# Hybrid decoder trunk on one core: gates and branch projections with tokens as rows of the product, merged rows transposed on TensorE

## The chip, the cores and the metric

One core of a Trainium2 chip runs the whole kernel. The metric is device time in microseconds (us) from launch to end. The kernel before takes 838.35 us (median of 3 runs, 837.55 to 838.98).

## The reference, cut to what matters

Two layers, 256 tokens, width 1024, float32. Each layer computes

```
h = rms_norm(x, g_pre_mix)
(a_u, a_v, b_q, b_k, b_v, c_b, c_c, c_x, d_cq, d_ckv, d_kr, gate_logits) = split_columns(h @ w_in)
out_a, out_b, out_c, out_d = four branches, each 256 tokens x 256 features
gates = sigmoid(gate_logits.reshape(b, s, 4, 1024))
merged = sum over i of gates[:, :, i, :] * (branches[i] @ w_branch[i])
x = x + rms_norm(merged @ w_out, g_post_mix)
h = rms_norm(x, g_pre_mlp)
x = x + rms_norm(square(relu(h @ w_mlp_in)) @ w_mlp_out, g_post_mlp)
```

`w_in` has 6496 columns, of which the last 4096 are the gate logits.

## The kernel before, in words

**Chunks.** All weights stream through one ring in chunks of 128 partitions x 2048 values (1 MB; 4 to 7 have 704 values), 68 a layer. A chunk comes in two halves of 512 KB: SyncE's queue loads a half into one of four `raw` slots, ScalarE copies it to `w_hi` rounded to the fast float32 format (`split_half`, L412), VectorE writes the remainder `raw - w_hi` to `w_lo` (L661). The ring of `w_hi`/`w_lo` holds 4 chunks, so ScalarE may start chunk c+4 only when TensorE has finished chunk c (`chunk_used`), and a raw slot is loaded again when its `w_lo` is done.

**Products.** A product (`product`, L1059) is three matmuls: hi by hi (L1062), hi by lo (L1063), lo by hi (L1064). In `matmul(dst, lhs, rhs)` lhs is the stationary operand (a 128x128 weight load of its own), rhs the moving one, whose columns are the columns of the result. Two forms are used. *Feature-major* (`feature_major`, L1084): weights are stationary, the 256 tokens move; a chunk is 16 products of 256 columns. *Token-major*: a tile of 128 tokens is stationary and 512 weight columns move; a chunk is 8 products of 512 columns.

**Order in a layer.** Chunks 0 to 3 and 4 to 7 are input projections, token-major. 8 to 11 are feature-major projections. 12 to 27 are the gates, feature-major: 4 chunks for each branch, 2 x 128 gate channels a chunk, in PSUM banks 6 and 7 in turn, each read by one `Tanh` (`gate_tanh`, L452). Between these chunks the branches' own small work is put in (`side_after` on TensorE after chunk c, `side_step(l, s)` on ScalarE and VectorE). Chunks 28 to 31 are the branch projections, one per branch: 4 *units* a chunk, unit u being 2 x 128 output channels by 256 tokens, in bank 4+u. Chunks 32 to 35 are `w_out`, token-major, first all four for token tile t=0 (48 matmuls), then all four for t=1. Then the MLP.

**The merge.** Sigmoid is written as (tanh(z/2)+1)/2. For each of the 16 units VectorE computes (tanh+1) * projection (`gate_unit`, L872), GpSimd adds it to `merged` (L1051), and for the last branch the sums are halved and split into `xT_hi` on ScalarE (L592) and `xT_lo` on VectorE (L887). As the units are feature-major, `merged` is already transposed and is what `w_out` needs as stationary operand. TensorE may write a unit's bank again when VectorE has read it (`unit_gated`).

**What sets the order.** Each engine has one queue written out by hand, with semaphore waits; nothing is planned or reordered at run time. VectorE's order around the merge is L910 to L938, ScalarE's L570 to L594.

Of the kernel before, what the change touches and what calls it, by code (L numbers as in the profile page):

```python
# [21 lines left out]
def hybrid_trunk(nc: bass.Bass, x_in: bass.AP, g_pre_mix: bass.AP, w_in: bass.AP, a_ln_g: bass.AP,  # L22
# [51 lines left out]
    with ExitStack() as ctx:  # L74
# [23 lines left out]
        gated = proj.rearrange("p t (u n) -> p (t u) n", u=2)  # L98
# [4 lines left out]
        merged = rows.rearrange("p (u n) -> p u n", u=4)  # L103
# [163 lines left out]


# [62 lines left out]
        def _(sp):  # L331
# [79 lines left out]
        def _(act):  # L411
# [60 lines left out]
            def side_step(l, s):  # L472
                if s == 4:
# [67 lines left out]
                if C_GATE < s <= C_BRANCH:  # L541
                    gate_tanh(l, s - C_GATE - 1)
# [3 lines left out]
            with act.Fori(0, L) as l:  # L546
# [23 lines left out]
                for s in range(4, C_OUT):  # L570
# [87 lines left out]
        def _(dve):  # L658
# [83 lines left out]
            def side_step(l, s):  # L742
# [688 lines left out]
```

## Time and profile before

| | |
|---|---|
| median of 3 runs | 838.35 us |
| profiled execution: span | 836.2 us |
| outside the span | 2.2 us (median less span; the profiled execution has no other time of its own) |
| TensorE busy (matmuls) | 817.1 us, 98% |
| VectorE busy | 485.3 us, 58% |
| ScalarE busy | 404.1 us, 48% |
| GpSimd busy | 66.3 us, 8% |
| DMA | 146.67 MB, mean 175 GB/s |
| granted TensorE clock | full in all but the starts of the two layers |

How to read it: matmuls are pipelined, so each is shown longer than the time that it adds; what one costs is the distance from its start to the start of the next. `x3` at a line's end counts the instructions merged in it. An operand pair in the third column reads out<-moving,stationary. The second layer repeats the first 412.7 us later.

### The profile page before, as it was taken

Reading aid. Unit: us, or ns where it says so; the run is one execution under the profiler, and the core shown is the slowest. Engines: PE = TensorE matmul, PEld = TensorE weight load, DVE = VectorE, ACT = ScalarE, POOL = GpSimd, SP = SyncE. Lnnn points to the kernel's source line nnn. Section 1 sums busy time; section 2 is a strip of 40 time slices with the busy share of each in tenths; the row PEclk is TensorE's granted clock in tenths of the full one; section 3 lists DMA queues with packets and bytes.
Section 4 is the critical chain, followed back from the end, with each engine's and each line's share of the span. In section 5 each row is a group of like instructions: output and inputs, shape, how many; then the busy total and the mean of one; then the engine's idle time right before and its main releaser. Section 6 shows DMA issues by size and latency. Waiting matters only on the chain.

```text
span 836.2 us, 15189 instructions
## 1 busy us (share of the span) xinstructions
PE 817.1 (98%) x5598; PEld 753.7 (90%) x5598; DVE 485.3 (58%) x621; ACT 404.1 (48%) x623; POOL 66.3 (8%) x95
## 2 busy tenths in 40 slices
PE   7999999999999999999989999999999999999997
PEld 6898999999789999999878999999988999999995
DVE  4577444439786555555374774444597765555553
ACT  4565554443465444444264645454335654444432
POOL 2010000004410000000010100000072100000000
PEclk9999999999999999999999999999999999999999
DMA  8787455565367555565347864545544666655531
GB/s 252 202 269 217 124 151 151 151 194 160 104 184 231 188 188 177 188 201 181 122 123 230 273 172 140 152 134 169 191 137 128 200 203 200 195 181 179 195 128 51
DMA packets 101826, 146.67 MB, mean 175 GB/s; under 512 B 4965, under 2 KB 83189, under 8 KB 101765
## 3 DMA queue, kind: packets, MB, share of 16 engines
q1 hardware_dynamic: 101572, 145.32, 56.0%
q8 instruction: 34, 0.56, 0.3%
q0 software_dynamic: 192, 0.57, 0.2%
q14 instruction: 28, 0.22, 0.1%
HBM read 144.83 MB, written 1.05 MB: 174 GB/s over the span
## 4 chain that ended last, share of the span: by engine, by line
PE 92%; DVE 2%; issue 2%; DMA 1%; ACT 1%; POOL 1%; DVEq 0%; SPq 0%; ACTq 0%; POOLq 0%
PE banks L1062 29%; PE banks L1063 28%; PE banks L1064 28%; DMA raw<-in_w_in_dram 1%; PE banks L1124 1%; PE banks L1074 1%; PE banks L1132 1%; DVE proj L884 1%; PE banks L1123 1%; DVE w_lo L666 1%; PE banks L1192 0%; PE banks L1149 0%; PE banks L1148 0%; PE banks L1204 0%; PE banks L1189 0%
## 5 line engine op out<-in xcount | busy, mean ns | idle before, releaser
L666 DVE TENSOR_TENSOR w_lo<-raw,w_hi 128x1024 fp32r<-128x1024 f32 (+1 forms) x272 | 319.2, 1209 | 163.0 <-ACT w_hi L419 162.0
L419 ACT CAST w_hi<-raw 128x1024 fp32r<-128x1024 f32 (+1 forms) x272 | 264.0, 1012 | 131.7 <-PE banks L1064 90.3
L1062 PE MATMUL banks<-xT_hi,w_hi 128*128 128x256 f32 x1088 | 310.8, 286 | 0.0
L1064 PE MATMUL banks<-xT_hi,w_lo 128*128 128x256 f32 x1088 | 307.8, 283 | 0.0
L1063 PE MATMUL banks<-xT_lo,w_hi 128*128 128x256 f32 x1088 | 307.8, 283 | 0.0
L1062 PEld LDWEIGHTS banks<-xT_hi,w_hi 128*128 128x128 f32 x1088 | 208.5, 192 | 2.1 <-issue 1.1
L1063 PEld LDWEIGHTS banks<-xT_lo,w_hi 128*128 128x128 f32 x1088 | 208.6, 192 | 1.5 <-issue 0.5
L1064 PEld LDWEIGHTS banks<-xT_hi,w_lo 128*128 128x128 f32 x1088 | 208.5, 192 | 0.0
L1062 PE MATMUL banks<-w_hi,brT_hi 128*128 128x512 f32 x256 | 100.0, 390 | 0.0
L1063 PE MATMUL banks<-w_lo,brT_hi 128*128 128x512 f32 x256 | 99.9, 390 | 0.0
L1064 PE MATMUL banks<-w_hi,brT_lo 128*128 128x512 f32 x256 | 99.6, 389 | 0.0
L1062 PE MATMUL banks<-w_hi,xT_hi 128*128 128x512 f32 (+2 forms) x224 | 80.9, 361 | 6.5 <-DVE xT_lo L685 4.1
L1063 PE MATMUL banks<-w_lo,xT_hi 128*128 128x512 f32 (+2 forms) x224 | 79.0, 353 | 0.0
L1064 PE MATMUL banks<-w_hi,xT_lo 128*128 128x512 f32 (+2 forms) x224 | 78.9, 352 | 0.0
L631 ACT ACTIVATE rows<-banks 128x512 f32<-128x512 f32 x32 | 19.1, 596 | 108.1 <-PE banks L1064 104.0
L964 DVE TENSOR_TENSOR rows<-rows 128x512 f32<-128x512 f32 x32 | 22.1, 692 | 84.4 <-ACT rows L631 84.2
L1064 PEld LDWEIGHTS banks<-w_hi,brT_lo 128*128 128x128 f32 x256 | 48.1, 188 | 10.2
L1051 POOL TENSOR_TENSOR rows<-rows,proj 128x512 f32<-128x512 f32 x22 | 34.3, 1596 | 284.8 <-DVE proj L884 284.8
L1062 PEld LDWEIGHTS banks<-w_hi,brT_hi 128*128 128x128 f32 x256 | 48.2, 188 | 9.2
L1063 PEld LDWEIGHTS banks<-w_lo,brT_hi 128*128 128x128 f32 x256 | 48.2, 188 | 9.0
L1062 PEld LDWEIGHTS banks<-w_hi,xT_hi 128*128 128x128 f32 x224 | 42.7, 191 | 14.7 <-DVE w_lo L666 4.7
L1064 PEld LDWEIGHTS banks<-w_hi,xT_lo 128*128 128x128 f32 x224 | 42.7, 191 | 5.3
(174 smaller groups left out, 722.8 us busy)
## 6 DMA issues: line engine op xcount, KB each, us to landing
raw<-in_w_in_dram SPq DMA_DIRECT2D x96, 512.0 KB, 4.5
raw<-in_w_mlp_in_dram SPq DMA_DIRECT2D x64, 512.0 KB, 3.9
raw<-in_w_mlp_out_dram SPq DMA_DIRECT2D x64, 512.0 KB, 4.3
raw<-in_w_branch_dram SPq DMA_DIRECT2D x16, 512.0 KB, 4.0
raw<-in_w_out_dram SPq DMA_DIRECT2D x16, 512.0 KB, 3.9
raw<-in_w_in_dram SPq DMA_DIRECT2D x16, 176.0 KB, 2.4
gain_pre<-in_g_pre_mix_dram SPq DMA_DIRECT2D x2, 512.0 KB, 4.5
gain_pre<-in_g_pre_mlp_dram SPq DMA_DIRECT2D x2, 512.0 KB, 5.8
```

Of the source, the lines that this page charges most:

```text
L419: nc.scalar.copy(w_hi[:, c % RING, h * n:(h + 1) * n], raw[:, q % RAW, 0:n]).then_inc(hi_ready, 1)
L631: nc.scalar.activation(hidden_relu[:, k % 2, :], psum[:, bank, :], ACT.Relu).then_inc(relu_ready, 1)
L666: v.tensor_tensor(w_lo[:, c % RING, cut], raw[:, q % RAW, 0:n], w_hi[:, c % RING, cut].bitcast(F32), ALU.subtract).then_inc(lo_ready, 1)
L884: v.scalar_tensor_tensor(dst, gate_v[:, i, u, :], 1.0, psum[:, 4 + u, :], ALU.add, ALU.mult).then_inc(unit_gated, 1)
L964: v.tensor_tensor(hidden_sq, hidden_relu[:, k % 2, :], hidden_relu[:, k % 2, :], ALU.mult).then_inc(hidden_squared, 1)
L1051: g.tensor_tensor(merged[:, u, :], merged[:, u, :], gated[:, u, :], ALU.add).then_inc(unit_added, 1)
L1062: nc.tensor.matmul(dst, l_hi, r_hi, start=first, stop=False)
L1063: nc.tensor.matmul(dst, l_hi, r_lo, start=False, stop=False)
L1064: return nc.tensor.matmul(dst, l_lo, r_hi, start=False, stop=last)
L1074: last = nc.tensor.transpose(psum[:, 4 + 2 * t + b, j * P:(j + 1) * P], xn[:, t, kt * P:(kt + 1) * P], ident)
L1123: nc.tensor.matmul(psum[:, h % 2, 0:P], q[:, 0:P], k[:, 0:P], start=True, stop=True)
L1124: nc.tensor.matmul(psum[:, h % 2, P:3 * P], q[:, P:S], k, start=True, stop=True).then_inc(scores_psum, 1)
```

## The change

The ring, the chunk sizes and the set of products stay. The gate chunks 12 to 27 become token-major: a pair of chunks (input channels 0 to 511, then 512 to 1023) gives 512 gate columns for both token tiles, tile t in bank 6+t, read by one `Tanh` a tile. The branch projections become token-major: a unit is now (branch i, token tile t, half h of the 1024 columns), 6 matmuls of 512 columns. `UNITS` puts branches 0 and 1 first in full, then branches 2 and 3 for t=0, then for t=1. The gated product is written over the tanh in place. GpSimd adds branches 1 and 2; VectorE adds branch 3 (`add_last`). `merged` now has tokens on its partitions, so TensorE transposes it in 16 pieces of 128x128 a layer (`transpose_merged`): 8 after unit 13, 8 before the last `w_out` chunk of t=0. ScalarE and VectorE read the transposes from PSUM (`merged_hi`, `merged_lo`), 4 of 512 columns each, as before. The orders of VectorE and ScalarE around the merge are rewritten.

```diff
--- before.py
+++ after.py
+UNITS = [(i, t, h) for i in range(2) for t in range(T) for h in range(2)]
+UNITS += [(i, t, h) for t in range(T) for i in range(2, NB) for h in range(2)]
+FREES_CHUNK = [UNITS.index(u) for u in ((0, 1, 1), (1, 1, 1), (2, 1, 1), (3, 1, 1))]
+UNIT_PSUM = [n for n in range(len(UNITS)) if n not in FREES_CHUNK]
+assert len(UNITS) == 16
...
@@ -282,7 +289,7 @@
 def shape_of(c):

-    if c < C_D:
+    if c < C_D or C_GATE <= c < C_BRANCH:
...
         for c in range(C_GATE, C_BRANCH):
-            col = COL_GATE + 256 * (c - C_GATE)
-            load(l, c, w_in_v[l, :, :, col:col + 256])
+            g, kh = (c - C_GATE) // 2, (c - C_GATE) % 2
+            col = COL_GATE + 512 * g
+            load(l, c, w_in_v[l, :, 4 * kh:4 * kh + 4, col:col + 512])
...
@@ -449,10 +457,20 @@

-    def gate_tanh(l, g):
-        act.wait_ge(chunk_used, used(l, C_GATE + g))
-        nc.scalar.activation(gate_v[:, g // 4, g % 4, :], psum[:, 6 + g % 2, :], ACT.Tanh,
+    def gate_tanh(l, g, t):
+        if t == 0:
+            act.wait_ge(gate_psum, nth(l, 8, g))
+        else:
+            act.wait_ge(chunk_used, used(l, C_GATE + 2 * g + 1))
+        nc.scalar.activation(gate_v[:, g // 2, 2 * t + g % 2, :], psum[:, 6 + t, :], ACT.Tanh,
+    def merged_hi(l, t):
+        for b in range(2):
+            act.wait_ge(mergedT_psum, nth(l, 4, 2 * t + b))
+            nc.scalar.activation(xT_hi[:, 4 * b:4 * b + 4, t * P:(t + 1) * P],
+                                 psum[:, 2 + 2 * t + b, :].rearrange("p (k n) -> p k n", k=4),
+                                 ACT.Copy, scale=0.5).then_inc(mergedT_hi_ready, 1)
     def head_exp(l, h):
...
@@ -538,8 +558,8 @@
             branch_hi(l, (1, 3)[n], psum[:, 4, :])
-        if C_GATE < s <= C_BRANCH:
-            gate_tanh(l, s - C_GATE - 1)
+        if C_GATE < s <= C_BRANCH and (s - C_GATE) % 2 == 0:
+            gate_tanh(l, (s - C_GATE) // 2 - 1, 1)
...
@@ -584,14 +604,13 @@

-        for u in range(4):
-            if u == 0:
-                act.wait_ge(unit0_added, nth(l, 1, 0))
-            else:
-                act.wait_ge(unit_added, nth(l, 11, 7 + u))
-            nc.scalar.activation(xT_hi[:, 2 * u:2 * u + 2, :].rearrange("p k n -> p (k n)"),
-                                 merged[:, u, :], ACT.Copy, scale=0.5).then_inc(mergedT_hi_ready, 1)
+        split(l, C_OUT)
+        split(l, C_OUT + 1)
+        split_half(l, C_OUT + 2, 0)
+        merged_hi(l, 0)
+        split_half(l, C_OUT + 2, 1)
         split(l, C_OUT + 3)
+        merged_hi(l, 1)
...
-            dve.wait_ge(unit_psum, nth(l, 12, 3 * i + u))
+    def gate_unit(l, n):
+        i, t, h = UNITS[n]
+        if n in FREES_CHUNK:
+            dve.wait_ge(chunk_used, used(l, C_BRANCH + i))
         else:
-            dve.wait_ge(chunk_used, used(l, C_BRANCH + i))
-        if i == 0:
+            dve.wait_ge(unit_psum, nth(l, 12, UNIT_PSUM.index(n)))
+        if n == 0:
             dve.wait_ge(gate_ready, nth(l, 16, 15))
-        if i >= 2:
-            dve.wait_ge(unit_added, nth(l, 11, 4 * (i - 2) + u))
-        dst = merged[:, u, :] if i == 0 else gated[:, u, :]
-        v.scalar_tensor_tensor(dst, gate_v[:, i, u, :], 1.0, psum[:, 4 + u, :], ALU.add, ALU.mult
-                               ).then_inc(unit_gated, 1)
-    def merged_lo(l, u):
-        dve.wait_ge(mergedT_hi_ready, nth(l, 4, u))
-        flat = "p k n -> p (k n)"
-        v.scalar_tensor_tensor(xT_lo[:, 2 * u:2 * u + 2, :].rearrange(flat), merged[:, u, :], 0.5,
-                               xT_hi[:, 2 * u:2 * u + 2, :].rearrange(flat).bitcast(F32),
-                               ALU.mult, ALU.subtract).then_inc(mergedT_lo_ready, 1)
+        gate = gate_v[:, i, 2 * t + h, :]
+        v.scalar_tensor_tensor(merged[:, 2 * t + h, :] if i == 0 else gate, gate, 1.0,
+                               psum[:, 4 + n % 4, :], ALU.add, ALU.mult).then_inc(unit_gated, 1)
+    def add_last(l, t, h):
+        dve.wait_ge(unit_gated, nth(l, 16, UNITS.index((3, t, h))))
+        dve.wait_ge(unit_added, nth(l, 8, 4 + 2 * t + h))
+        j = 2 * t + h
+        v.tensor_tensor(merged[:, j, :], merged[:, j, :], gate_v[:, 3, j, :], ALU.add
+                        ).then_inc(merged_ready, 1)
+    def merged_lo(l, t):
+        for b in range(2):
+            dve.wait_ge(mergedT_hi_ready, nth(l, 4, 2 * t + b))
+            cut = slice(t * P, (t + 1) * P)
+            v.scalar_tensor_tensor(xT_lo[:, 4 * b:4 * b + 4, cut],
+                                   psum[:, 2 + 2 * t + b, :].rearrange("p (k n) -> p k n", k=4), 0.5,
+                                   xT_hi[:, 4 * b:4 * b + 4, cut].bitcast(F32),
+                                   ALU.mult, ALU.subtract).then_inc(mergedT_lo_ready, 1)
...
@@ -919,23 +943,32 @@
                 split(l, s + 3)
-        side_step(l, C_OUT - 1)
+        for n in range(4):
+            gate_unit(l, n)
+        split_half(l, C_OUT, 0)
+        gate_unit(l, 4)
+        split_half(l, C_OUT, 1)
+        for n in range(5, 8):
+            gate_unit(l, n)
+        split_half(l, C_OUT + 1, 0)
+        gate_unit(l, 8)
+        split_half(l, C_OUT + 1, 1)
+        for n in range(9, 12):
+            gate_unit(l, n)
+        add_last(l, 0, 0)
+        add_last(l, 0, 1)
+        gate_unit(l, 12)
+        gate_unit(l, 13)
+        merged_lo(l, 0)
-        gate_unit(l, NB - 1, 0)
-        dve.wait_ge(unit_gated, nth(l, 16, 12))
-        dve.wait_ge(unit_added, nth(l, 11, 4))
-        v.tensor_tensor(merged[:, 0, :], merged[:, 0, :], gated[:, 0, :], ALU.add).then_inc(unit0_added, 1)
-        gate_unit(l, NB - 1, 1)
-        merged_lo(l, 0)
-        gate_unit(l, NB - 1, 2)
-        gate_unit(l, NB - 1, 3)
+        gate_unit(l, 14)
+        gate_unit(l, 15)
+        add_last(l, 1, 0)
+        add_last(l, 1, 1)
+        split_half(l, C_OUT + 2, 1)
+        split(l, C_OUT + 3)
         merged_lo(l, 1)
-        split_half(l, C_OUT + 2, 1)
-        merged_lo(l, 2)
-        merged_lo(l, 3)
-        split(l, C_OUT + 3)
...
@@ -1043,12 +1076,12 @@
                         minus_half, ALU.pow).then_inc(rstdD_ready, 1)
-        for i in range(1, NB):
-            for u in range(1 if i == NB - 1 else 0, 4):
-                pool.wait_ge(unit_gated, nth(l, 16, 4 * i + u))
+        for i in range(1, NB - 1):
+            for j in range(4):
+                pool.wait_ge(unit_gated, nth(l, 16, UNITS.index((i, j // 2, j % 2))))
                 if i > 1:
-                    pool.wait_ge(unit_added, nth(l, 11, 4 * (i - 2) + u))
-                g.tensor_tensor(merged[:, u, :], merged[:, u, :], gated[:, u, :], ALU.add
+                    pool.wait_ge(unit_added, nth(l, 8, 4 * (i - 2) + j))
+                g.tensor_tensor(merged[:, j, :], merged[:, j, :], gate_v[:, i, j, :], ALU.add
...
@@ -1074,6 +1107,14 @@
+    def transpose_merged(l, t):
+        for b in range(2):
+            pe.wait_ge(merged_ready, nth(l, 4, 2 * t + b))
+            for j in range(4):
+                last = nc.tensor.transpose(psum[:, 2 + 2 * t + b, j * P:(j + 1) * P],
+                                           merged[:, 2 * t + b, j * P:(j + 1) * P], ident)
+            last.then_inc(mergedT_psum, 1)
     def xT(kt, cut=slice(0, S)):
...
@@ -1280,31 +1321,39 @@
         for c in range(C_GATE, C_BRANCH):
-            n = c - C_GATE
+            g, kh = (c - C_GATE) // 2, (c - C_GATE) % 2
             wait_chunk(l, c)
-            if n >= 2:
-                pe.wait_ge(gate_ready, nth(l, 16, n - 2))
-            feature_major(l, c, 6 + n % 2).then_inc(chunk_used, 1)
+            hi, lo = both(c)
+            for t in range(T):
+                if kh == 0 and g >= 1:
+                    pe.wait_ge(gate_ready, nth(l, 16, 2 * (g - 1) + t))
+                for j in range(4):
+                    kt = 4 * kh + j
+                    last = product(psum[:, 6 + t, :], xT(kt, tokens(t)), (hi[:, j, :], lo[:, j, :]),
+                                   kt == 0, kt == KT - 1)
+                if kh == 1 and t == 0:
+                    last.then_inc(gate_psum, 1)
+            last.then_inc(chunk_used, 1)
             side_after(l, c)
-        for i in range(NB):
+        for n, (i, t, h) in enumerate(UNITS):
             c = C_BRANCH + i
-            wait_chunk(l, c)
-            if i == 0:
+            if (t, h) == (0, 0):
+                wait_chunk(l, c)
+            if n == 0:
                 pe.wait_ge(brT_lo_ready, nth(l, 4, ORDER_D))
+            if n >= 4:
+                pe.wait_ge(unit_gated, nth(l, 16, n - 4))
+            elif n >= 2:
+                pe.wait_ge(gate_ready, nth(l, 16, 12 + n))
             hi, lo = both(c)
-            for u in range(4):
-                if i >= 1:
-                    pe.wait_ge(unit_gated, nth(l, 16, 4 * (i - 1) + u))
-                elif u >= 2:
-                    pe.wait_ge(gate_ready, nth(l, 16, 12 + u))
-                for f in range(2):
-                    cut = slice((2 * u + f) * P, (2 * u + f + 1) * P)
-                    for kt in range(FT):
-                        last = product(psum[:, 4 + u, f * S:(f + 1) * S], (hi[:, kt, cut], lo[:, kt, cut]),
-                                       (brT_hi[:, FT * i + kt, :], brT_lo[:, FT * i + kt, :]),
-                                       kt == 0, kt == FT - 1)
-                last.then_inc(unit_psum if u < 3 else chunk_used, 1)
+            for kt in range(FT):
+                b = FT * i + kt
+                last = product(psum[:, 4 + n % 4, :], (brT_hi[:, b, tokens(t)], brT_lo[:, b, tokens(t)]),
+                               (hi[:, kt, columns(h)], lo[:, kt, columns(h)]), kt == 0, kt == FT - 1)
+            last.then_inc(chunk_used if n in FREES_CHUNK else unit_psum, 1)
+            if n == 13:
+                transpose_merged(l, 0)
         def output(l, c, t, h):
@@ -1316,12 +1365,17 @@
             wait_chunk(l, c)
-            pe.wait_ge(mergedT_lo_ready, nth(l, 4, c - C_OUT))
+            if (c - C_OUT) % 2 == 0:
+                pe.wait_ge(mergedT_lo_ready, nth(l, 4, (c - C_OUT) // 2))
+            if c == C_MLP - 1:
+                transpose_merged(l, 1)
         for c in range(C_OUT, C_MLP):
+            if (c - C_OUT) % 2 == 0:
+                pe.wait_ge(mergedT_lo_ready, nth(l, 4, 2 + (c - C_OUT) // 2))
...
```

## Rows read from the trace of the kernel before

**Rows 1.** The page's busy time by engine and the chain of waits by engine

```profile
PE 817.1 (98%) x5598; PEld 753.7 (90%) x5598; DVE 485.3 (58%) x621; ACT 404.1 (48%) x623; POOL 66.3 (8%) x95
...
PE 92%; DVE 2%; issue 2%; DMA 1%; ACT 1%; POOL 1%; DVEq 0%; SPq 0%; ACTq 0%; POOLq 0%
```

**Rows 2.** Waits of TensorE: waiter <- releaser: us in total, times, longest

```profile
PE banks L1062 <- DVE xT_lo L890: 2.2, 2, 1.1
PE banks L1062 <- DVE proj L884: 1.0, 2, 0.5
```

**Rows 3.** Timeline of TensorE, gate stage (start us, us, engine, line, op)

```profile
164.78 0.28 PE L1062 MATMUL banks<-xT_hi,w_hi 128*128 128x256 f32 x1
...
177.02 0.28 PE L1062 MATMUL banks<-xT_hi,w_hi 128*128 128x256 f32 x1
...
186.74 0.28 PE L1062 MATMUL banks<-brT_hi,w_hi 128*128 128x256 f32 x1
```

**Rows 4.** Timeline of TensorE, input projection, chunks 0 to 3

```profile
22.21 0.39 PE L1063 MATMUL banks<-w_lo,xT_hi 128*128 128x512 f32 x1
...
35.81 0.39 PE L1063 MATMUL banks<-w_lo,xT_hi 128*128 128x512 f32 x1
```

**Rows 5.** Timeline of TensorE, MLP loop: one chunk of either form

```profile
261.03 0.28 PE L1062 MATMUL banks<-xT_hi,w_hi 128*128 128x256 f32 x1
...
266.78 0.40 PE L1062 MATMUL banks<-w_hi,brT_hi 128*128 128x512 f32 x1
...
272.25 0.28 PE L1062 MATMUL banks<-xT_hi,w_hi 128*128 128x256 f32 x1
```

**Rows 6.** Timeline of TensorE, from unit 11's end to the second token tile

```profile
203.90 0.28 PE L1064 MATMUL banks<-brT_hi,w_lo 128*128 128x256 f32 x1
204.69 0.36 PE L1062 MATMUL banks<-brT_hi,w_hi 128*128 128x256 f32 x1 [0.51 <-DVE proj L884]
...
210.39 0.28 PE L1064 MATMUL banks<-brT_hi,w_lo 128*128 128x256 f32 x1
211.80 0.50 PE L1062 MATMUL banks<-w_hi,xT_hi 128*128 128x512 f32 x1 [1.12 <-DVE xT_lo L890]
...
223.32 0.39 PE L1062 MATMUL banks<-w_hi,xT_hi 128*128 128x512 f32 x1
```

**Rows 7.** Timeline of TensorE, eight transposes among matmuls

```profile
231.25 0.40 PE L1064 MATMUL banks<-w_hi,xT_lo 128*128 128x512 f32 x1
231.49 1.04 PE L1074 MATMUL banks<-ident,rows 128*128 128x128 f32 x8
232.28 0.47 PE L1062 MATMUL banks<-w_hi,xT_hi 128*128 128x512 f32 x1
232.59 0.39 PE L1063 MATMUL banks<-w_lo,xT_hi 128*128 128x512 f32 x1
```

**Rows 8.** Timeline of VectorE around the merge

```profile
188.50 2.36 DVE L666 TENSOR_TENSOR w_lo<-raw,w_hi 128x1024 fp32r<-128x1024 f32 x2 [3.40 <-ACT w_hi L419]
190.78 2.61 DVE L884 SCALAR_TENSOR_TENSOR rows<-gate_th,banks 128x512 f32<-128x512 f32 x4
...
199.54 4.40 DVE L666 TENSOR_TENSOR w_lo<-raw,w_hi 128x1024 fp32r<-128x1024 f32 x2 [0.39 <-ACT w_hi L419]
...
208.97 1.08 DVE L929 TENSOR_TENSOR rows<-rows,proj 128x512 f32<-128x512 f32 x1
```

**Rows 9.** GpSimd's adds (line's view: min/median/max ns) and VectorE's reads of transposes

```profile
L1051 POOL TENSOR_TENSOR rows<-rows,proj x22: 1290/1306/2291, 196.8 to 626.8; 128x512 f32<-128x512 f32 x22
...
L685 DVE TENSOR_TENSOR xT_lo<-banks,xT_hi x16: 679/684/693, 13.1 to 656.1; 128x512 fp32r<-128x512 f32 x16
```

**Rows 10.** Timeline of TensorE and ScalarE, start of chunk 14 and its Tanh

```profile
90.55 0.39 PE L1062 MATMUL banks<-xT_hi,w_hi 128*128 128x256 f32 x1
...
92.82 0.57 ACT L454 ACTIVATE gate_th<-banks 128x512 f32<-128x512 f32 x1
```

**Rows 11.** Windows of TensorE before layer 2: us, busy (instructions), PEclk, DMA, GB/s

```profile
419.00:424.00 5.00, 2.30 (x22) 1.00 0.03 8
424.00:428.00 4.00, 4.00 (x20) 0.57 0.25 54
```

More of the change, by code:

```diff
@@ L97, in hybrid_trunk @@
         proj = sb("proj", [P, T, 4 * MIX])
-        gated = proj.rearrange("p t (u n) -> p (t u) n", u=2)
         hidden_rows = proj
@@ L102, in hybrid_trunk @@
         xn = rows.rearrange("p (t d) -> p t d", t=T)
-        merged = rows.rearrange("p (u n) -> p u n", u=4)
+        merged = rows.rearrange("p (j n) -> p j n", j=4)
         qD = rows[:, 0:T * HEADS * QK].rearrange("p (t h e) -> p t h e", t=T, h=HEADS)
@@ L243, in hybrid_trunk @@
         gate_ready = sem("gate_ready")
+        gate_psum = sem("gate_psum")
         unit_psum = sem("unit_psum")
@@ L246, in hybrid_trunk @@
         unit_added = sem("unit_added")
-        unit0_added = sem("unit0_added")
+        merged_ready = sem("merged_ready")
+        mergedT_psum = sem("mergedT_psum")
         mergedT_hi_ready = sem("mergedT_hi_ready")
@@ L472, in side_step @@
             def side_step(l, s):
+                if C_GATE < s <= C_BRANCH and (s - C_GATE) % 2 == 0:
+                    gate_tanh(l, (s - C_GATE) // 2 - 1, 0)
                 if s == 4:
@@ L540, in side_step @@
                     branch_hi(l, (1, 3)[n], psum[:, 4, :])
-                if C_GATE < s <= C_BRANCH:
-                    gate_tanh(l, s - C_GATE - 1)
+                if C_GATE < s <= C_BRANCH and (s - C_GATE) % 2 == 0:
+                    gate_tanh(l, (s - C_GATE) // 2 - 1, 1)
             x_squares(0, 0, 0)
@@ L568, in _ @@
                         split(l, 5)
-                for s in range(4, C_OUT):
+                for s in range(4, C_BRANCH + 1):
                     if s in (5, 6):
@@ L867, in side_step @@
                     branch_lo(l, (1, 3)[n], (ORDER_B, ORDER_D)[n], psum[:, 4, :])
-                if C_BRANCH < s <= C_OUT:
-                    for u in range(4):
-                        gate_unit(l, s - C_BRANCH - 1, u)
-            def gate_unit(l, i, u):
-                if u < 3:
-                    dve.wait_ge(unit_psum, nth(l, 12, 3 * i + u))
-                else:
-                    dve.wait_ge(chunk_used, used(l, C_BRANCH + i))
-                if i == 0:
+            def gate_unit(l, n):
+                i, t, h = UNITS[n]
+                if n in FREES_CHUNK:
+                    dve.wait_ge(chunk_used, used(l, C_BRANCH + i))
+                else:
+                    dve.wait_ge(unit_psum, nth(l, 12, UNIT_PSUM.index(n)))
+                if n == 0:
@@ L908, in _ @@
                 dve.wait_ge(tables_landed, 16)
-                for s in range(4, C_OUT - 1):
+                for s in range(4, C_BRANCH + 1):
                     if s in (5, 6):
@@ L1295, in _ @@
                     hi, lo = both(c)
-                    for u in range(4):
-                        if i >= 1:
-                            pe.wait_ge(unit_gated, nth(l, 16, 4 * (i - 1) + u))
-                        elif u >= 2:
-                            pe.wait_ge(gate_ready, nth(l, 16, 12 + u))
-                        for f in range(2):
-                            cut = slice((2 * u + f) * P, (2 * u + f + 1) * P)
-                            for kt in range(FT):
-                                last = product(psum[:, 4 + u, f * S:(f + 1) * S], (hi[:, kt, cut], lo[:, kt, cut]),
-                                               (brT_hi[:, FT * i + kt, :], brT_lo[:, FT * i + kt, :]),
-                                               kt == 0, kt == FT - 1)
-                        last.then_inc(unit_psum if u < 3 else chunk_used, 1)
+                    for kt in range(FT):
+                        b = FT * i + kt
+                        last = product(psum[:, 4 + n % 4, :], (brT_hi[:, b, tokens(t)], brT_lo[:, b, tokens(t)]),
+                                       (hi[:, kt, columns(h)], lo[:, kt, columns(h)]), kt == 0, kt == FT - 1)
```

## The prediction

> **What bounds the kernel now.** I read the page first: TensorE is busy 98% of the span and holds 92% of the chain that ended last; no other engine passes 58% [rows 1]. So only two things can move the time: how long TensorE's stream is, and where it stands still. The view of its waits gives the second. Of those in the part that is edited there are two a run for `xT_lo` from `merged` (2.2 us) and two for a gated unit (1.0 us) [rows 2]; in the gates there is none. The first needs the timeline, since the durations of matmuls overlap: the distance between starts is the price. In the gate stage 102 matmuls of 256 columns lie between 164.78 and 177.02: 0.120 us each, 5.76 us for a chunk of 48 [rows 3]. With 512 columns moving, 60 lie between 22.21 and 35.81: 0.2267 us each, 5.44 us for a chunk of 24 [rows 4]. The MLP loop has both side by side: 5.75 us for a feature-major chunk, 5.47 us for a token-major one [rows 5]. Same columns, same products, half the instructions: about 0.013 us less for each two that become one. The granted clock is full there, its 2.4 GHz level.
>
> **The gates.** 16 chunks a layer go from 5.76 to between 5.44 and 5.47 us. I take 0.30 us each, near the middle: 4.8 us a layer; ends 4.5 and 5.1. The transfer is as large as before, and its runs are longer; TensorE has no wait for data in this stage, so I cost the loads at nothing. The new thing is that a bank is wanted sooner. In an odd chunk tile 0 is finished at half time, so its `Tanh` has 2.7 us before that bank is wanted. Tile 1's is issued only at the end of ScalarE's step, behind the head's exponentials, and TensorE wants the bank 12 matmuls into the next chunk. The tightest is step 14: the chunk starts at 90.55, tile 1 of it would start 12 x 0.227 later, at 93.27, and that `Tanh` ends at 92.82 + 0.57 = 93.39 [rows 10]. With the signal that is a wait of 0.2 us. If the step were a microsecond late it would be 1.2; in the other even steps the `Tanh` runs earlier against its chunk. What queues behind that `Tanh` on ScalarE is the copy of chunk 17, wanted three chunks later. Gates: 4.6 us gained a layer.
>
> The Trainium skill has a rule that speaks against this. "TensorE: Matmul & The Clock Gate", Back-to-back issue gap, gives columns/2.4 GHz + 2.5 ns for matmuls back to back: 109 ns for 256 columns, 216 for 512, so two made one would save 2.5 ns, not 13. By it the sum would shrink to some 0.06 us a chunk. The same section gives a measured 131 ns at 512 columns among weight loads. This trace agrees with neither: 120 and 227 ns.
>
> **From the first unit to the second token tile.** Before: unit 0 starts at 186.74 [rows 3], the second token tile at 223.32 [rows 6], 36.58 us. Of it 16 units of 12 x 0.120 are 23.04 us, the first tile's 48 matmuls of 0.2267 are 10.88 us, and 2.66 us is standing still: 0.67 before unit 12 (203.90 + 0.12 to 204.69), 1.29 before `w_out` (210.39 + 0.12 to 211.80), 0.70 in pieces behind chunk waits and `merged_lo` [rows 6].
>
> After: 16 units of 6 x 0.2267 are 21.76 us, 10.88 stays, and 16 transposes come. Eight of them took 0.79 us from 231.49 to 232.28, and the matmul behind them 0.31 instead of 0.23 [rows 7]: 0.87 us, twice 1.74. That is a floor of 34.4 us, if TensorE never waits.
>
> For its waits I ran the new orders by hand, from unit 0 as time 0. Prices: a gated unit 0.65 us and a half chunk's remainder 1.2 us on VectorE (2.61/4, 2.36/2), but 2.1 to 2.3 us with GpSimd adding (4.40 for two); an add on VectorE beside GpSimd 1.08 us [rows 8]; GpSimd's add 1.3 us alone and 2.3 against VectorE; a read of transposes by VectorE 0.68 us [rows 9].
> - VectorE finishes chunk 31 at 4.0 (190.78 - 186.74), as before, gates units 0 to 3 until 6.6, half a chunk to 7.9, unit 4 to 8.6. There GpSimd starts.
> - The half chunks after that cost 2.1: unit 7 is gated at 12.7, unit 8 at 15.4, unit 9 at 18.1, unit 11 at 19.4. Unit 13 may start when unit 9 is gated; TensorE is there at 17.8: wait 0.4.
> - GpSimd's sixth add ends near 19.7. The two `add_last` end at 20.3 and 21.0; TensorE has finished unit 13 at 19.7 and stands 1.0 us around the first eight transposes. Behind `add_last` on VectorE stand the gatings of units 12 and 13, wanted only by GpSimd, which has until 28.
> - TensorE: units 14 and 15 end at 24.3. `merged_lo` of tile 0 is ready at 23.3, so the 1.29 us stall is gone. Next late is chunk 34: its second half is done at 29.9, wanted at 29.8: wait 0.1 to 0.3. Chunk 35 (32.3) is in time, the last transposes wait for nothing, and their copies have a 2.7 us chunk over them.
>
> The waits come to 1.7 us; 34.4 + 1.7 = 36.1, against 36.6: 0.5 us gained a layer. Bounds: no wait at all gains 2.2; every half chunk and add at its dear price makes the waits 3.4 and loses 1.2.
>
> Why half chunks and adds stretch each other has a rule in the Trainium skill too ("SBUF — State Buffer", Who interferes with whom: VectorE and GpSimd share one pair of ports under an exclusive lock). The trace agrees: 2.1 to 2.3 instead of 1.2 us. By it the adds now made on VectorE would wait for a whole GpSimd add.
>
> Behind it nothing changes: the first tile's norm chain starts at its last matmul as before and has three of the second tile's four chunks, 8.2 us, over it; the transposed x, the MLP and its starts are the same code.
>
> **The sum.** 4.6 + 0.5 = 5.1 us a layer, 10.2 us for two. The span goes from 836.2 to 826.0, and the median, 2.2 above the span, from 838.35 to 828.2 us.
>
> **The rivals.**
> 1. *The stream never waits in the merge.* If GpSimd's adds mostly cost 1.3, the median in [rows 9], the waits fall near 0. Layer 4.8 + 2.2 = 7.0 us; 824.4 us. Against it: VectorE's half chunks lie among the adds in the new order.
> 2. *GpSimd and VectorE become the bound (slower).* Place: the two `add_last` ahead of the first transposes. If each of GpSimd's six adds until then takes 2.3 us from 8.6 on, the sixth ends at 22.4 and two adds of 1.08 make it 24.6, 4.9 us after unit 13. A stand of that size also lowers the clock: after a gap of 2.7 us the grant was 0.57 over the next 4 us, the 1.2 GHz level most of the time [rows 11], which costs 1.7 us. The excess over my 1.0 is 3.9 + 1.7 = 5.6 us a layer against 5.1 gained, and each wait behind it adds: with 1 us more late in chunks 34 and 35 the run takes 838.35 + 2 x 1.5 = 841.4. It decides where standing and slowed clock together pass 6.1 us a layer. For it: one add did take 2.29. Against it: the median is 1.31 [rows 9].
> 3. *512 columns cost twice 256 in this place.* As if 0.240: gates and units gain nothing, the merge loses 1.74 for transposes and keeps some 1.2 of waits against 2.66: +0.3, chunk 14 +0.2, twice: 839.4 us. This is what the skill's N/2.4 rule comes near to. Against it: rows 4 and 5 are the same form with the same operands, in three stages.
> 4. *The early Tanh or the data is late in each gate chunk.* 0.3 us a chunk would eat the gates' gain: 837 us. Against it: ScalarE is busy 48% of the span [rows 1], and apart from step 14 its work stays where it was.
>
> **How the numbers follow.** Forecast 0.76, its own range 825.5 to 831.5 (gates 4.3 to 4.9, merge -0.9 to +1.6). Rival 1: 0.14. Rival 2: 0.05, of it 0.03 slower and 0.01 within. Rival 3: 0.02. Rival 4: 0.03. A measurement of this kernel tells 0.2%, 1.7 us, from no change. Rivals 3 and 4 lie within it. Faster 0.76 + 0.14 + 0.01 = 0.91, same 0.01 + 0.02 + 0.03 = 0.06, slower 0.03. The range takes rival 1 in and, above, a merge that loses 1.2 a layer: 4.5 - 0.7 - 1.2 = 2.6, twice 5.2, 833.1. So 823.8 to 833.
>
> **What would show it.** Right: starts 0.227 us apart in the gates and gate chunks of 5.44 to 5.47 us; one short wait in chunk 14; eight transposes twice a layer at 0.87 us; from the first unit to the second tile 35 to 37 us; layers 5 us shorter each. Wrong: starts 0.24 apart, or the first column of waits led by TensorE <- `add_last` with more than 2 us a layer, or a granted clock below full around it.

## The result, and the profile after

The changed kernel takes 827.71 us (median of 4 runs, 827.31 to 828.51); the kernel before takes 838.66 us beside it (4 runs). The ratio is 0.9874, 95% interval 0.9861 to 0.9887: 10.9 us, 1.3% faster. Forecast was 828.2.

The page of the changed kernel, busy time by engine and chain by engine, answers to [rows 1]: TensorE still bounds it, with 928 fewer matmuls. Line numbers are those of the changed kernel: `product` is L1095 to L1097, `transpose_merged` L1115, `gate_unit` L898, `add_last` L906.

```profile
PE 808.6 (98%) x4670; PEld 705.8 (85%) x4670; DVE 483.7 (59%) x627; ACT 405.8 (49%) x623; POOL 58.2 (7%) x89
...
PE 93%; issue 2%; DVE 2%; DMA 1%; POOL 1%; ACT 1%; DVEq 0%; SPq 0%; ACTq 0%; POOLq 0%
```

TensorE's waits after, all of them (waiter <- releaser, us in total, times, longest). Both waits of [rows 2] are gone; in their place stands one for `add_last` before the first transposes.

```profile
PE banks L1107 <- DVE rows L697: 6.1, 4, 3.5
PE banks L1095 <- DVE xT_lo L704: 3.0, 3, 2.2
PE banks L1138 <- POOL causal L1040: 2.5, 1, 2.5
PE banks L1115 <- DVE rows L906: 0.9, 2, 0.5
```

**Gates.** Timeline of TensorE in the last gate chunks of the changed kernel, up to unit 0 at 183.50: 42 matmuls of 512 columns in 9.52 us, 0.2267 us each, the distance of [rows 4] and not twice the 0.120 of [rows 3].

```profile
173.98 0.39 PE L1095 MATMUL banks<-w_hi,xT_hi 128*128 128x512 f32 x1
...
183.50 0.39 PE L1095 MATMUL banks<-w_hi,brT_hi 128*128 128x512 f32 x1
```

Where the gate stage starts, in the kernel before and then in the changed one (one fence each). Before, from 76.35 to 186.74 [rows 3], it is 110.39 us. After, from 77.45 to 183.50, 106.05: **4.34 us less a layer**.

```profile
76.35 0.28 PE L1062 MATMUL banks<-xT_hi,w_hi 128*128 128x256 f32 x1
```

```profile
77.45 0.40 PE L1095 MATMUL banks<-w_hi,xT_hi 128*128 128x512 f32 x1
```

**Merge.** The same timeline from unit 13's end on, which answers to [rows 6] and [rows 7]: unit 13 ends at 202.31 + 0.23 = 202.54, the transposes start 0.63 us later and have a further 0.23 us inside them (203.17 to 204.19 against 0.79 us for the second eight, 215.17 to 215.96); `w_out` starts at 207.00 with no gap behind unit 15.

```profile
202.31 0.39 PE L1097 MATMUL banks<-w_hi,brT_lo 128*128 128x512 f32 x1
203.17 1.26 PE L1115 MATMUL banks<-ident,rows 128*128 128x128 f32 x8 [0.47 <-DVE rows L906]
204.19 0.48 PE L1095 MATMUL banks<-w_hi,brT_hi 128*128 128x512 f32 x1
...
206.78 0.39 PE L1097 MATMUL banks<-w_hi,brT_lo 128*128 128x512 f32 x1
207.00 0.39 PE L1095 MATMUL banks<-w_hi,xT_hi 128*128 128x512 f32 x1
...
215.17 1.03 PE L1115 MATMUL banks<-ident,rows 128*128 128x128 f32 x8
215.96 0.48 PE L1095 MATMUL banks<-w_hi,xT_hi 128*128 128x512 f32 x1
...
218.78 0.39 PE L1095 MATMUL banks<-w_hi,xT_hi 128*128 128x512 f32 x1
...
226.94 1.03 PE L1107 MATMUL banks<-ident,rows 128*128 128x128 f32 x8
```

From unit 0 to the second token tile it is 218.78 - 183.50 = 35.28 us, against 36.58: **1.30 us less a layer**. The wider units give 1.28 us of it (23.04 to 21.76), the waits 1.76 (2.66 to 0.90), and the transposes take 1.74. A mark that every kernel below has is the first transposes of the normed x, 8.2 us further on: from unit 0 to them it was 231.49 - 186.74 = 44.75 us [rows 3, 7] and is 226.94 - 183.50 = 43.44. I call this the merge distance.

### The profile page after: what moved, and what is told of

It is laid out like the page before. It is cut to its first block, busy times and chain, and to the rows that moved or that the text cites. A ratio compares the mean times of both kernels' runs of the same rounds, so it can differ in the third digit from the quotient of the medians.

```text
span 826.7 us, 13275 instructions
## 1 busy us (share of the span) xinstructions
PE 808.6 (98%) x4670; PEld 705.8 (85%) x4670; DVE 483.7 (59%) x627; ACT 405.8 (49%) x623; POOL 58.2 (7%) x89
## 4 chain that ended last, share of the span: by engine, by line
PE 93%; issue 2%; DVE 2%; DMA 1%; POOL 1%; ACT 1%; DVEq 0%; SPq 0%; ACTq 0%; POOLq 0%
PE banks L1095 29%; PE banks L1096 28%; PE banks L1097 28%; DMA raw<-in_w_in_dram 1%; PE banks L1165 1%; PE banks L1107 1%; PE banks L1173 1%; PE banks L1164 1%; PE banks L1115 1%; DVE gate_th L898 0%; PE banks L1233 0%; PE banks L1190 0%; PE banks L1189 0%; PE banks L1245 0%; POOL rstd L1053 0%
## 5 line engine op out<-in xcount | busy, mean ns | idle before, releaser
L685 DVE TENSOR_TENSOR w_lo<-raw,w_hi 128x1024 fp32r<-128x1024 f32 (+1 forms) x272 | 316.1, 1198 | 153.2 <-ACT w_hi L427 151.9
L1095 PE MATMUL banks<-w_hi,xT_hi 128*128 128x512 f32 (+2 forms) x480 | 182.7, 381 | 3.0 <-DVE xT_lo L704 3.0
L1096 PE MATMUL banks<-w_lo,xT_hi 128*128 128x512 f32 (+2 forms) x480 | 178.9, 373 | 0.0
L1097 PE MATMUL banks<-w_hi,xT_lo 128*128 128x512 f32 (+2 forms) x480 | 178.9, 373 | 0.0
L1095 PE MATMUL banks<-xT_hi,w_hi 128*128 128x256 f32 x576 | 164.0, 285 | 0.0
L1097 PE MATMUL banks<-xT_hi,w_lo 128*128 128x256 f32 x576 | 163.0, 283 | 0.0
L1096 PE MATMUL banks<-xT_lo,w_hi 128*128 128x256 f32 x576 | 163.0, 283 | 0.0
L1095 PE MATMUL banks<-w_hi,brT_hi 128*128 128x512 f32 x320 | 125.0, 391 | 0.0
L1097 PE MATMUL banks<-w_hi,brT_lo 128*128 128x512 f32 x320 | 124.5, 389 | 0.0
L1096 PEld LDWEIGHTS banks<-xT_lo,w_hi 128*128 128x128 f32 x576 | 110.4, 192 | 1.5 <-issue 0.5
L1095 PEld LDWEIGHTS banks<-xT_hi,w_hi 128*128 128x128 f32 x576 | 110.4, 192 | 1.5 <-issue 0.5
L1097 PEld LDWEIGHTS banks<-xT_hi,w_lo 128*128 128x128 f32 x576 | 110.4, 192 | 0.0
L1095 PEld LDWEIGHTS banks<-w_hi,xT_hi 128*128 128x128 f32 x480 | 91.0, 190 | 19.1 <-DVE w_lo L685 2.4
L1097 PEld LDWEIGHTS banks<-w_hi,xT_lo 128*128 128x128 f32 x480 | 90.9, 189 | 15.8
L1096 PEld LDWEIGHTS banks<-w_lo,xT_hi 128*128 128x128 f32 x480 | 91.1, 190 | 14.2
L1097 PEld LDWEIGHTS banks<-w_hi,brT_lo 128*128 128x128 f32 x320 | 60.1, 188 | 12.7
L1095 PEld LDWEIGHTS banks<-w_hi,brT_hi 128*128 128x128 f32 x320 | 60.2, 188 | 11.7
```

Of the source, the lines that this page charges most:

```text
L685: v.tensor_tensor(w_lo[:, c % RING, cut], raw[:, q % RAW, 0:n], w_hi[:, c % RING, cut].bitcast(F32), ALU.subtract).then_inc(lo_ready, 1)
L1095: nc.tensor.matmul(dst, l_hi, r_hi, start=first, stop=False)
L1096: nc.tensor.matmul(dst, l_hi, r_lo, start=False, stop=False)
L1097: return nc.tensor.matmul(dst, l_lo, r_hi, start=False, stop=last)
```

## The experiments

Each kernel was timed beside the kernel before (838.4 to 838.7 us). The merge distance is read from the timeline of layer 1; in layer 2 it is the same within 0.1 us except where the table says otherwise.

| kernel | median us | ratio to before, 95% | merge distance us |
|---|---|---|---|
| changed | 827.71 | 0.9874, 0.9861 to 0.9887 | 43.44 |
| gates_only | 829.2 | 0.989, 0.9874 to 0.9907 | 44.70 |
| merge_only | 836.75 | 0.9979, 0.9969 to 0.9988 | 43.54 |
| gates_256 | 836.3 | 0.9978, 0.9968 to 0.9988 | 43.51 |
| transposes_twice | 831.14 | 0.9915, 0.9898 to 0.9931 | 45.04 |
| transposes_later | 826.15 | 0.9856, 0.9841 to 0.9871 | 42.85 |
| gpsimd_one_column | 825.6 | 0.9846, 0.9832 to 0.9859 | 42.61 |
| gpsimd_branch2_twice | 837.19 | 0.9983, 0.9972 to 0.9993 | 47.63 (layer 2: 48.75) |
| gates_128 | 995.15 | 1.1861, 1.1842 to 1.1879 | 43.55 |
| changed_again | 828.23 | 0.9872, 0.9854 to 0.9889 | 43.50 |
| later_again | 826.35 | 0.9855, 0.9837 to 0.9872 | 42.85 |

### Which part gives how much: gates_only and merge_only

gates_only is the kernel before with `shape_of`, the loads, `gate_tanh`, `side_step` and the gate loop of the changed kernel; merge_only is the changed kernel with these parts of the kernel before. The core of gates_only:

```diff
-                    feature_major(l, c, 6 + n % 2).then_inc(chunk_used, 1)
+                            last = product(psum[:, 6 + t, :], xT(kt, tokens(t)), (hi[:, j, :], lo[:, j, :]),
+                                           kt == 0, kt == KT - 1)
```

> Only the gate chunks 12 to 27 are token-major; branch units, merge and their orders are those of before (the gate values then meet other elements of the projections, so the merged sum is not the reference's; the work is the same). Theory: what is saved is 0.0133 us for each two 256-column matmuls that become one of 512, so this part alone carries most of the gain: gate stage 106.0 us instead of 110.4, 4.3 us a layer, 8.7 us in all, near 829.8 us. Rival: the gain comes from the stalls of the merge; then this run stays near 836.

> Only the branch units, the merge, its transposes and the orders around it are those of the change; the gates are feature-major as before (gate values meet other elements, so the merged sum is not the reference's). Theory: 1.3 us a layer from the first unit to the second token tile (36.6 to 35.3 us), 2.6 us in all, near 836.0 us; with gates_only the two savings add up to the whole. Rival: the merge part gives nothing or costs (transposes 1.74 us a layer not paid for), 838.5 or more.

gates_only is 9.3 us faster than before, merge_only 1.8; together 11.1, the whole is 10.9. So most of the gain is in the gates, and the rival (the stalls of the merge carry it) falls. gates_only still has both waits of [rows 2], here with 2.3 and 1.0 us. merge_only missed by 0.75 us: its merge distance fell by 1.21 us a layer, nearly the 1.3 expected, and the longer start of layer 2 (last section) more than covers the rest.

### Is it the columns in one instruction: gates_256 and gates_128

gates_256 is shown; gates_128 has four parts of 128 columns.

```diff
-                            last = product(psum[:, 6 + t, :], xT(kt, tokens(t)), (hi[:, j, :], lo[:, j, :]),
-                                           kt == 0, kt == KT - 1)
+                            for q in range(2):
+                                cols = slice(256 * q, 256 * q + 256)
+                                last = product(psum[:, 6 + t, cols], xT(kt, tokens(t)),
+                                               (hi[:, j, cols], lo[:, j, cols]),
+                                               kt == 0 and q == 0, kt == KT - 1 and q == 1)
```

> The changed kernel, but each gate matmul of 512 columns is issued as two of 256 with the same stationary operand (same order, banks, transfers). Theory (columns in one instruction): starts 0.120 us apart again, gate chunks 5.76 us, the gates' 8.7 us are given back: near 836.4 us. Rival (token-major order, stationary x, or longer transfers are what helps): stays near 827.7.

> The changed kernel, with each gate matmul of 512 columns issued as four of 128 with the same stationary operand. It asks what the fixed part of a matmul is. Theory A (a constant 0.0133 us on top of the columns at 2.4 GHz): starts 0.067 us apart, a gate chunk 6.4 us instead of 5.44, 32 chunks, near 858 us. Theory B (below 256 columns something else binds, such as the weight load in front of every matmul, of which eight transposes of 128 columns took 0.79 us): starts about 0.10 us apart, a chunk 9.5 us, near 958 us.

gates_256 gives back 8.6 of the 10.9 us; order, banks, stationary operand and transfers are those of the changed kernel. Each of its halves brings a weight load of its own, as every matmul here does, so the run doesn't tell whether the 0.0133 us belong to the matmul or to its load. Its timeline: 41 matmuls in 4.92 us, 0.120 us each.

```profile
164.72 0.28 PE L1095 MATMUL banks<-w_hi,xT_hi 128*128 128x256 f32 x1
...
169.64 0.28 PE L1097 MATMUL banks<-w_hi,xT_lo 128*128 128x256 f32 x1
```

gates_128 lies beyond both theories. TensorE and its weight loads in a gate chunk there: 15 matmuls of 128 columns in 1.68 us, 0.112 us each, and 14 weight loads in 1.56 us, 0.111 each. One matmul of 256 columns takes hardly longer than one of 128.

```profile
154.74 0.28 PE L1095 MATMUL banks<-w_hi,xT_hi 128*128 128x128 f32 x1
...
156.42 0.28 PE L1095 MATMUL banks<-w_hi,xT_hi 128*128 128x128 f32 x1
```

```profile
154.91 0.19 PEld L1097 LDWEIGHTS banks<-w_hi,xT_lo 128*128 128x128 f32 x1
...
156.47 0.19 PEld L1096 LDWEIGHTS banks<-w_lo,xT_hi 128*128 128x128 f32 x1
```

So the distance is 0.2267 us at 512 columns and 0.120 at 256, which both are the columns at 2.4 GHz plus 0.0133 us. At 128 that would be 0.067 and something else sets 0.111. Theory B had the kind right and the size low: 96 x 0.1114 = 10.7 us a chunk, 5.25 more than 5.44, and 32 chunks give 168 us; measured are 167.4. That it is the weight load is argued from its equal pace, not shown by a run without it. "TensorE: Matmul & The Clock Gate", LDWEIGHTS, of the Trainium skill puts a weight load of 128 columns at 107 ns; the trace agrees with it nearly.

### What the transposes cost: transposes_twice

```diff
-                    for j in range(4):
+                    for j in (0, 1, 2, 3, 0, 1, 2, 3):
```

> The changed kernel, with each of the 16 transposes of merged a layer done twice. Theory (transposes lie on TensorE's stream and nothing hides them): 32 more at 0.10 us, less some 0.1 us a layer that fall into the wait for the second add: plus 3.0 us, near 830.7. Rival (they lie in the wait for the adds): plus 1.5 us or less.

3.4 us more than the changed kernel. Unit 0, the first transposes and those of x:

```profile
181.97 0.39 PE L1095 MATMUL banks<-w_hi,brT_hi 128*128 128x512 f32 x1
...
201.65 1.97 PE L1115 MATMUL banks<-ident,rows 128*128 128x128 f32 x16 [0.47 <-DVE rows L906]
...
227.01 1.03 PE L1107 MATMUL banks<-ident,rows 128*128 128x128 f32 x8
```

The merge distance is 45.04 us, 1.60 more for 16 transposes. Sixteen in a row before the last `w_out` chunk take 1.66 us (214.37 to 216.03), 0.109 each and 0.87 more than eight; the sixteen behind unit 13 take 1.72 (201.65 to 203.37), only 0.70 more than the 1.02 of the changed kernel, as the wait for the second add, which lay among the eight, falls into them. So nothing hides the transposes but some 0.2 us of that wait. The token-major form needs these transposes; the 5.6 us won in a layer are what is left after 1.7 paid for them.

### What the stand before them is: transposes_later and gpsimd_one_column

transposes_later, then gpsimd_one_column:

```diff
-                    if n == 13:
+                    if n == 14:
                         transpose_merged(l, 0)
...
-                        g.tensor_tensor(merged[:, j, :], merged[:, j, :], gate_v[:, i, j, :], ALU.add
+                        g.tensor_tensor(merged[:, j, 0:1], merged[:, j, 0:1], gate_v[:, i, j, 0:1], ALU.add
```

> The changed kernel, with the first eight transposes of merged put behind unit 14 instead of unit 13 on TensorE. Theory (the 0.63 us stand before them is the wait for GpSimd's and VectorE's last adds, and unit 14 is ready to run in it): the stand goes, nothing is late behind it (merged_lo of tile 0 has unit 15 over it): 0.6 us a layer, 1.2 us in all, near 826.5 us. Rival: the stand moves to the first w_out chunk, as merged_lo is late there by about the same: 827.7.

> The changed kernel, with GpSimd adding one column instead of 512 in each of its 8 adds a layer (branches 1 and 2 are left out of the sum elsewhere). Theory (GpSimd's adds and what they cost VectorE beside them set the stand before the transposes): VectorE's half chunks fall from 1.7 to 2.3 us to 1.2, the stand of 0.63 us goes, 0.6 us a layer, near 826.5 us. Rival (VectorE's own order sets it): the stand stays, 827.7.

The theory holds in both, in the first not for the whole 0.86 us of standing (0.63 and 0.23). TensorE in the first, then in the second:

```profile
182.16 0.39 PE L1095 MATMUL banks<-w_hi,brT_hi 128*128 128x512 f32 x1
...
202.57 1.03 PE L1115 MATMUL banks<-ident,rows 128*128 128x128 f32 x8
...
225.01 1.03 PE L1107 MATMUL banks<-ident,rows 128*128 128x128 f32 x8
```

```profile
182.46 0.39 PE L1095 MATMUL banks<-w_hi,brT_hi 128*128 128x512 f32 x1
...
201.50 1.04 PE L1115 MATMUL banks<-ident,rows 128*128 128x128 f32 x8
...
225.07 1.03 PE L1107 MATMUL banks<-ident,rows 128*128 128x128 f32 x8
```

202.57 - 182.16 is 20.41 us: 15 units of 1.36. 201.50 - 182.46 is 19.04: 14 units. Neither has a stand before the transposes, and the merge distances fall by 0.59 and 0.83 us. In transposes_later some 0.2 us come back in front of chunk 34, the third of `w_out`: the matmul before it and its own first one take 0.31 and 0.34 us to the next instead of 0.23. VectorE finishes that chunk's second half, the first of the three below, only at about 210.3. This is the wait that the prediction expected for chunk 34.

```profile
210.06 0.39 PE L1097 MATMUL banks<-w_hi,xT_lo 128*128 128x512 f32 x1
210.37 0.50 PE L1095 MATMUL banks<-w_hi,xT_hi 128*128 128x512 f32 x1
```

```profile
209.10 3.48 DVE L685 TENSOR_TENSOR w_lo<-raw,w_hi 128x1024 fp32r<-128x1024 f32 x3
```

What GpSimd's adds do to VectorE is in VectorE's timeline of the changed kernel and then of gpsimd_one_column, half chunks (L685) and the two `add_last` (L906):

```profile
195.66 2.27 DVE L685 TENSOR_TENSOR w_lo<-raw,w_hi 128x1024 fp32r<-128x1024 f32 x1 [0.40 <-ACT w_hi L427]
...
198.45 1.72 DVE L685 TENSOR_TENSOR w_lo<-raw,w_hi 128x1024 fp32r<-128x1024 f32 x1
...
201.88 1.84 DVE L906 TENSOR_TENSOR rows<-rows,gate_th 128x512 f32<-128x512 f32 x2
```

```profile
194.62 1.23 DVE L685 TENSOR_TENSOR w_lo<-raw,w_hi 128x1024 fp32r<-128x1024 f32 x1 [0.40 <-ACT w_hi L427]
...
196.36 1.22 DVE L685 TENSOR_TENSOR w_lo<-raw,w_hi 128x1024 fp32r<-128x1024 f32 x1
...
199.58 1.29 DVE L906 TENSOR_TENSOR rows<-rows,gate_th 128x512 f32<-128x512 f32 x2
```

2.27 and 1.72 us fall to 1.23 and 1.22, and the two `add_last` from 1.84 to 1.29. In the changed kernel VectorE works from 195.66 on without a pause up to the two `add_last`: its own work, stretched beside GpSimd, is what is late there. gpsimd_one_column takes away GpSimd's chain and the stretching together, so it doesn't price them one by one.

transposes_later leaves nothing out and is the fastest such version here. Beside the changed kernel:

> The changed kernel once more, on the same chip as the version with the later transposes: 827.7 us by every theory; it is here so that the two are compared side by side.

> The changed kernel with the first eight transposes behind unit 14, a second time. Theory (the stand of 0.63 us a layer is saved and nothing else moves): 1.3 to 1.6 us under changed_again, near 826.2. Rival (the first difference was one between chips): no difference.

828.23 (826.9 to 828.39) and 826.35 us (825.88 to 827.14): 1.9 us, more than the 1.3 to 1.6 expected; the merge distances account for 1.2 to 1.3. The two intervals against the kernel before overlap, so it is both pairs (1.6 us between different chips, 1.9 side by side) and the timelines that show that the move helps; the size is read from the trace, 0.6 us a layer.

### Rival 2 made to happen: gpsimd_branch2_twice

```diff
+                        if i == 2:
+                            spare = hidden_rows[:, j // 2, 512 * (j % 2):512 * (j % 2) + 512]
+                            g.tensor_tensor(spare, merged[:, j, :], gate_v[:, i, j, :], ALU.add)
```

> The changed kernel, with each of GpSimd's four adds of branch 2 done twice a layer (once into a spare tile). Theory (GpSimd's chain is already the last thing in front of the first transposes): two more adds of 1.3 to 1.7 us ahead of them put 2.6 to 3.4 us on the stand, a layer 3 us longer, near 833.7 us; if the stand of 3.6 us also lowers the granted clock after it, up to 837. Rival (there is room in GpSimd's chain): under 1 us in all.

Two more adds ahead of the first transposes cost 4.19 us of merge distance in layer 1 and 5.31 in layer 2, 9.5 us in all: nearly the whole gain, and the upper of the two times expected (837). TensorE's timeline in layer 1 and then its windows in both layers (us, busy, instructions, granted clock, DMA share, GB/s):

```profile
203.68 0.66 PE L1118 MATMUL banks<-ident,rows 128*128 128x128 f32 x4 [1.70 <-DVE rows L906]
205.60 0.66 PE L1118 MATMUL banks<-ident,rows 128*128 128x128 f32 x4 [1.26 <-DVE rows L906]
```

```profile
204.00:208.00 4.00, 2.74 (x14) 0.82 0.01 2
208.00:212.00 4.00, 4.00 (x14) 0.75 0.18 38
...
616.00:620.00 4.00, 2.75 (x9) 0.52 0.00 0
620.00:624.00 4.00, 4.00 (x13) 0.62 0.24 70
```

Unit 13 ends at 182.78 + 19.04 = 201.82. The first four transposes start 1.86 us later and the second four 1.92 after them, where 0.44 is what four take: 3.34 us of standing, 2.5 more than the 0.86 of the changed kernel. The rest is the clock: two windows of 4 us at a mean grant of 0.82 and 0.75, a share of each at the 1.2 GHz level, lose 0.72 + 1.0 = 1.7 us (an estimate; between 206.94 and 209.92 the matmuls start 0.427 us apart, which is 512 columns at 1.2 GHz). 2.5 + 1.7 is the 4.2 measured. In layer 2 the standing is the same, but the grants are 0.52 and 0.62 and the matmuls stay 0.427 us apart until 622.9: there the clock takes 5.31 - 2.5 = 2.8 us. So rival 2's mechanism, both halves, is real. In the changed kernel the stand is 0.86 us and the grant stays at 1.00 from 200 to 212 us, so its second half wasn't reached. But its GpSimd chain has only about half a microsecond to spare: the sixth add ends at 202.57 (192.12 + 10.45, below), the second `add_last` starts at about 203.0, and two more adds put 2.5 us on the stand.

## Why the prediction was right

**The price of 512 columns** (0.2267 against twice 0.120 us) was right to the digit, and gates_256 shows it to be the cause. Rival 3 falls; so does what the N/2.4 rule of the Trainium skill would have made of it, as "TensorE: Matmul & The Clock Gate", Back-to-back issue gap, has 2.5 ns where the trace has 13.3. For a stream in which every matmul has its weight load, as here, the section itself sets that rule aside and gives 131 ns at 512 columns, which the 226.7 ns measured here don't bear out either.

**Gates: 4.6 forecast, 4.34 measured.** The wait of chunk 14 was sized 0.2 us and is 0.04. TensorE there, first the chunk's start, with 0.34 us to the second matmul, then 0.27 us instead of 0.23 where the second tile begins; below it the `Tanh` that it waits for:

```profile
91.07 0.50 PE L1095 MATMUL banks<-w_hi,xT_hi 128*128 128x512 f32 x1
91.41 0.39 PE L1096 MATMUL banks<-w_lo,xT_hi 128*128 128x512 f32 x1
...
93.70 0.39 PE L1097 MATMUL banks<-w_hi,xT_lo 128*128 128x512 f32 x1
93.97 0.50 PE L1095 MATMUL banks<-w_hi,xT_hi 128*128 128x512 f32 x1
```

```profile
93.34 0.58 ACT L465 ACTIVATE gate_th<-banks 128x512 f32<-128x512 f32 x1
```

The `Tanh` ends at 93.92, 2.85 us behind the chunk's start, as in the forecast (93.39 - 90.55). But the chunk's first half, 12 x 0.227 = 2.7 us in the forecast, took 2.9 from 91.07, so it wanted the bank later. The step that was sized wrong is the price of a chunk: I took the steady distance for all chunks, but the first six or so matmuls behind side work, or behind a wait, stand 0.23 to 0.34 us apart. Chunks 25 to 27, which follow no side work, took 5.44 us (before: 5.76, 0.32 more). Those from 15 to 24 took 5.54 to 5.57 (before: mostly 5.83 to 5.84, 0.26 to 0.29 more), and chunk 14, which has two such starts, 5.75 (before: 5.86, only 0.11 more). So chunk 14 gave 0.2 us less than the 0.30 forecast for each, which is what was taken off for its wait, but the wait was 0.04 of it: that number came out by luck. The other 0.26 us are missing mostly in chunks 15 to 24. Rival 4 did not occur.

**Merge: 0.5 forecast, 1.30 measured.** The floor of 34.4 us was right; of the waits, sized 1.7 us, 0.90 came, 0.86 of it around the first transposes. Rival 1 had them at nothing: the truth lies midway. The step that failed is the price of VectorE beside GpSimd. I charged both sides of every meeting, but as far as these rows show only the one that starts second is stretched: the second half of chunk 32 took 1.22 us, not 2.1, and the GpSimd add that started after it (192.12) was the one to be stretched; GpSimd's first six adds took 10.45 us, where six alone are 7.8 (6 x 1.30). The three half chunks from there on, 2.1 us each in the forecast, took 1.22, 2.27 and 1.72. VectorE's and GpSimd's timelines:

```profile
191.96 1.22 DVE L685 TENSOR_TENSOR w_lo<-raw,w_hi 128x1024 fp32r<-128x1024 f32 x1
```

```profile
192.12 10.45 POOL L1084 TENSOR_TENSOR rows<-rows,gate_th 128x512 f32<-128x512 f32 x6 [134.72 <-DVE gate_th L898]
```

So units 8 and 9 were gated earlier (15.0 and 17.3 us after unit 0, not 15.4 and 18.1), the wait of 0.4 before unit 13 did not come, and neither did the one for chunk 34. The place of the remaining wait, its releaser and what it is made of were as forecast (1.0 against 0.86 us). One term of the range has no source: the 0.7 us taken off the gates in its upper end (4.5 - 0.7).

**What was not forecast** is a longer start of layer 2, 0.85 us at its first transposes. The prediction had "the MLP and its starts are the same code" and put it at nothing. 2 x (4.34 + 1.30) - 0.85 = 10.4 us, against 10.2 forecast and 10.9 measured. The median therefore agrees better than its parts, by luck: gates too high by 0.3 a layer, merge too low by 0.8, and one term missing. The spans of the two profiled executions differ by only 9.5 us (836.2 and 826.7), as layer 1's gates begin 1.1 us later in the changed one (77.45, not 76.35). That start varies from one execution to the next: the second eight transposes of layer 1 begin at 20.84 us there and at 19.99 in changed_again, the same kernel. The start of layer 2 varies too: from the last transposes of x in layer 1 to the second eight of layer 2 it is 190.83 us before, 191.37 in the changed kernel and 192.12 in changed_again, 0.5 and 1.3 more.

## What to carry to other kernels

When TensorE's stream is the bound and every matmul brings its own weight load, compare the distances between starts of both forms, not their durations: two matmuls of 256 columns made one of 512 gave 0.013 us, and here 40 chunks of 24 of them, 12.8 us, easily paid for 32 transposes of 0.10 us. Read the price of a form from a stage that has it already, and add the first few matmuls behind each interruption at their own price. A reordered merge is safe only as far as its slowest helper has room (two more GpSimd adds took nearly the whole gain): put the consumer of two engines' last adds behind one more piece of ready work.

## What the runs showed of the hardware

**A floor near 0.11 us for a matmul with its weight load.** Distances were 0.2267, 0.120 and 0.112 us for 512, 256 and 128 columns. From 256 to 128 columns hardly anything is saved. What sets the floor is not shown; the weight loads have the same pace (0.111 us).

**A stand of 3.3 us in two parts, four transposes between them, was followed by a lower clock, and not by the same amount each time.** In gpsimd_branch2_twice the grants from its second part on were 0.82 and 0.75 in layer 1 and 0.52 and 0.62 in layer 2 (means over 4 us each). After the changed kernel's stand of 0.86 us it stayed at 1.00.

**The loop start of layer 2 depends on the code.** In it TensorE waits for the first normalised rows. In the kernel before and in gates_only that wait is 2.70 and 2.77 us; in all ten profiles with the rewritten merge (every other kernel of the table) it is 3.40 to 3.70. TensorE in gates_only and in the changed kernel:

```profile
419.51 1.77 PE L1081 MATMUL banks<-ident,rows 128*128 128x128 f32 x8 [2.77 <-DVE rows L685]
```

```profile
420.28 1.45 PE L1107 MATMUL banks<-ident,rows 128*128 128x128 f32 x8 [3.55 <-DVE rows L697]
```

The row of VectorE that releases it has an idle time with no releaser in the profile ("issue"): 2.03 us before and 2.10 in gates_only, 2.83 to 3.10 in the ten; first of the kernel before, then of the changed one.

```profile
423.11 1.41 DVE L678 SCALAR_TENSOR_TENSOR rows<-x,rstd,gain_pre 128x512 f32<-128x512 f32 x2 [2.03 <-issue]
```

```profile
419.47 1.41 DVE L697 SCALAR_TENSOR_TENSOR rows<-x,rstd,gain_pre 128x512 f32<-128x512 f32 x2 [2.95 <-issue]
```

The MLP and the loop around it are the same code in both. As gates_only doesn't have the longer wait and merge_only does, it comes with the rewritten merge and not with the gates. What in the rewritten code costs this 0.85 us at the loop's return stays open: no run varied that alone.
